# First adaptive-norm slice and input loaded in four column pairs, with row sums in four column quarters of PE

## The reference

```
ada = silu(c) @ W_ada[l] + b_ada[l]          # W_ada[l] is 1024 x 6144
sh1, sc1, g1, sh2, sc2, g2 = split(ada, 6)
u = x * (1 + sc1) + sh1
x = LayerNorm(alpha * x + (1 + g1) * Mixer(u))
u = x * (1 + sc2) + sh2
x = LayerNorm(alpha * x + (1 + g2) * SwiGLU(u))
```

## Time and profile before

| | us |
|---|---|
| median of 3 runs | 1724.36 |
| profiled execution, its own time | 1726.44 |
| its span | 1724.6 |
| PE busy | 1665.3 (97%) |
| DVE busy | 1017.7 (59%) |
| ACT busy | 630.8 (37%) |
| bytes moved | 192.05 MB, 111 GB/s |

### The profile page before, as it was taken

How to read it: one execution, slowest core, us unless ns; L and a number is a source line. 1 busy time by engine, 2 the same in 40 slices (tenths; PEclk the granted TensorE clock), 3 DMA queues, 4 the chain that set the end, 5 groups by cost and what they waited for, 6 DMA issues and landing times.

```text
span 1724.6 us, 21810 instructions
## 1 busy us (share of the span) xinstructions
PE 1665.3 (97%) x8561; PEld 1328.8 (77%) x8561; DVE 1017.7 (59%) x1620; ACT 630.8 (37%) x1146; POOL 51.4 (3%) x100
## 2 busy tenths in 40 slices
PE   6899999999999999999999999999999999999997
PEld 5778766677787888888878776666778788888886
DVE  4767578767675555554567656777567533333344
ACT  0532344544343322222253324454533533222222
POOL 2000000000000000000000000000000000000000
PEclk9899999999999999999999999999999999999997
DMA  9464322124326666655426231111233233333331
GB/s 325 131 183 138 83 62 62 37 86 134 113 72 198 180 183 184 194 165 161 141 82 170 79 86 50 38 25 35 65 98 98 62 97 98 97 98 101 91 100 49
DMA packets 269685, 192.05 MB, mean 111 GB/s; under 512 B 8168, under 2 KB 254480, under 8 KB 268560
## 3 DMA queue, kind: packets, MB, share of 16 engines
q1 hardware_dynamic: 255632, 147.94, 29.4%
q0 software_dynamic: 12032, 42.07, 8.2%
q10 hardware_dynamic: 1920, 0.66, 0.2%
HBM read 188.54 MB, written 2.10 MB: 111 GB/s over the span
## 4 chain that ended last, share of the span: by engine, by line
PE 89%; DVE 5%; DMA 2%; ACT 2%; issue 1%; SPq 0%; ACTq 0%; DVEq 0%
PE banks L1460 24%; PE banks L1462 23%; PE banks L1461 23%; PE banks L1576 4%; PE banks L1604 3%; PE banks L1630 2%; PE banks L1509 1%; PE banks L1510 1%; PE banks L1511 1%; PE banks L1578 1%; DMA ring<-in_w_in_dram 1%; DMA ada_first_a<-in_w_ada_dram 1%; PE banks L1664 1%; DVE w_lo L891 1%; PE banks L1524 1%
## 5 line engine op out<-in xcount | busy, mean ns | idle before, releaser
L1460 PE MATMUL banks<-u_hi,w_hi 128*128 128x512 f32 x1216 | 500.0, 411 | 10.3 <-DVE w_lo L891 7.6
L891 DVE TENSOR_TENSOR w_lo<-ring,w_hi 128x1024 fp32r<-128x1024 f32 (+2 forms) x246 | 294.4, 1199 | 316.6 <-ACT w_hi L632 315.7
L1462 PE MATMUL banks<-u_hi,w_lo 128*128 128x512 f32 x1216 | 476.2, 392 | 0.0
L1461 PE MATMUL banks<-u_lo,w_hi 128*128 128x512 f32 x1216 | 476.0, 391 | 0.0
L632 ACT ACTIVATE w_hi<-ring 128x1024 fp32r<-128x1024 f32 (+2 forms) x246 | 253.8, 1032 | 234.2 <-PE banks L1462 98.6
L1460 PEld LDWEIGHTS banks<-u_hi,w_hi 128*128 128x128 f32 x1216 | 230.1, 189 | 53.0 <-DVE w_lo L891 8.9
L1462 PEld LDWEIGHTS banks<-u_hi,w_lo 128*128 128x128 f32 x1216 | 229.2, 188 | 49.4
L1461 PEld LDWEIGHTS banks<-u_lo,w_hi 128*128 128x128 f32 x1216 | 230.5, 190 | 36.8
L779 ACT ACTIVATE probs<-banks,neg_max 128x128 f32<-128x128 f32 (+3 forms) x192 | 99.5, 523 | 168.4 <-DVE neg_max L1247 168.4
L1460 PE MATMUL banks<-h_hi,w_hi 128*128 128x512 f32 x352 | 138.5, 394 | 0.0
L1462 PE MATMUL banks<-h_hi,w_lo 128*128 128x512 f32 x352 | 137.0, 389 | 0.0
(11 more groups left out here) (225 smaller groups left out, 2098.6 us busy)
## 6 DMA issues: line engine op xcount, KB each, us to landing
ring<-in_w_ffn_in_dram SPq DMA_DIRECT2D x88, 512.0 KB, 3.9
ada_ring<-in_w_ada_dram POOLq DMA_DIRECT2D x80, 512.0 KB, 4.2
ring<-in_w_in_dram SPq DMA_DIRECT2D x72, 512.0 KB, 3.8
ring<-in_w_ffn_out_dram SPq DMA_DIRECT2D x32, 448.0 KB, 3.6
ring<-in_w_out_dram SPq DMA_DIRECT2D x16, 512.0 KB, 3.9
ring<-in_w_ffn_out_dram SPq DMA_DIRECT2D x16, 512.0 KB, 4.4
ada_first_a<-in_w_ada_dram SPq DMA_DIRECT2D x5, 1024.0 KB, 9.1
w<-in_cmp_w_k_dram SPq DMA_DIRECT2D x8, 512.0 KB, 4.9
```

Of the source, the lines that this page charges most:

```text
L891: V.tensor_tensor(lo, src, hi.bitcast(fp32), ALU.subtract).then_inc(split_lo, 1)
L1460: M(bank, wh[:, block], sh[:, k, :], start=start, stop=False)
L1461: M(bank, wh[:, block], sl[:, k, :], start=False, stop=False)
L1462: return M(bank, wl[:, block], sh[:, k, :], start=False, stop=stop)
```

## The change

The first 2048 columns of W_ada[0] and x are no longer loaded by rows of W_ada, but by four pairs of chunks. Pair j is x's 256 columns of chunks 2j and 2j + 1, and for the shift and the scale the 256 columns that belong to them, in two halves of 512 rows. The rows of these transfers are 1 KB long. kc and vc are loaded behind pair 0, ksl behind pair 1, kwn behind pair 2. The bias of the first 2048 columns comes with c and is turned with it.

DVE sums no slices any more. PE multiplies by a padded silu(c): 32 columns of which the first is silu(c) of one row block and the others zero (c_pad). Row block k = 4 * half + g goes to the g-th quarter of PE's columns and of the bank's partitions, 512 columns wide. ACT copies the bank (first_rows), and four column products of one column each bring the sums onto partitions and add the quarters. DVE adds the bias for the pair, and the two chunks of u are made. PE takes kc, vc and ksl together, chunk by chunk (`first_products`), between the row sums of the next pair. The turning of the vectors moves behind the last of these products, and DVE's copies of them, with POOL's start signal ahead of them, behind the last chunk. x is turned in three banks instead of six. The job parts w1 are loaded behind other jobs than before, after and not ahead of them.

```diff
-    order = [(0, "ada01")] + [(l, name) for l in range(DEPTH) for name in CHUNKS if name not in THIRD]
+    order = [(l, name) for l in range(DEPTH) for name in CHUNKS if name not in THIRD]
-W1_WITH = ["vsg0", "vsg1", "vsg2", "qn0", "qn1", "qn2", "qn3", "kd0"]
+W1_WITH = ["vsg1", "vsg2", "qn0", "qn0", "qn1", "qn1", "qn2", "qn3"]
...
+            def load_pair(j):
+                part = slice(2 * P * j, 2 * P * (j + 1))
+                sp.dma_start(x_tok[:, :, part], x[0, :, part].rearrange("(i p) n -> p i n", p=P)).then_inc(x_in[j], 16)
+                for half in range(2):
+                    rows = w_ada[0, 4 * P * half:4 * P * (half + 1), :]
+                    for a in range(2):
+                        src = rows[:, D_MODEL * a + 2 * P * j:D_MODEL * a + 2 * P * (j + 1)]
+                        sp.dma_start(ada_first[j][:, 4 * half:4 * half + 4, 2 * P * a:2 * P * (a + 1)],
+                                     src.rearrange("(k p) n -> p k n", p=P)).then_inc(first_in[2 * j + half], 16)
...
-            for k in range(KD):
-                if k >= 3:
-                    sp.wait_ge(first_in[k - 3], 16)
-                if k == 6:
-                    sp.dma_start(x_tok, x[0].rearrange("(i p) n -> p i n", p=P)).then_inc(x_in, 16)
-                sp.dma_start(ada_first[k], w_ada[0, k * P:(k + 1) * P, 0:2 * D_MODEL]).then_inc(first_in[k], 16)
-            for name in JOBS[:NS]:
-                load(0, name)
+            load_pair(0)
+            load(0, JOBS[0])
+            load(0, JOBS[1])
+            load_pair(1)
+            load(0, JOBS[2])
+            load_pair(2)
+            load(0, JOBS[3])
+            load_pair(3)
...
-            prepare(0, "kc")
-            prepare(0, "vc")
-            act.wait_ge(part1, 1)
-            for k in range(KD):
-                act.wait_ge(x_saved, k + 1)
-                sub_layer_input(0, k, banks[:, 2 + k % 6, :], mul_u[:, 0, k:k + 1], ada[:, 0, k:k + 1])
-                if k == 3:
+            for j in range(PAIRS):
+                act.wait_ge(rows_summed, j + 1)
+                nc.scalar.activation(first_rows, rows_ps, ACT.Copy).then_inc(rows_saved, 1)
+                if j == 0:
+                    prepare(0, "kc")
+                act.wait_ge(pair_ready, j + 1)
+                for k in (2 * j, 2 * j + 1):
+                    act.wait_ge(x_saved, k + 1)
+                    sub_layer_input(0, k, banks[:, 2 + k % 3, :], mul_u[:, 0, k:k + 1], ada[:, 0, k:k + 1])
+                if j == 0:
+                    prepare(0, "vc")
                     prepare(0, "ksl")
...
+            def first_pair(j):
+                at = ada[:, 0, 0:2 * KD].rearrange("p (a k) -> p a k", a=2)[:, :, 2 * j:2 * j + 2]
+                bias = vec[:, 0, 0:2 * KD].rearrange("p (a k) -> p a k", a=2)[:, :, 2 * j:2 * j + 2]
+                dve.wait_ge(cols_summed, j + 1)
+                link(V.tensor_tensor(at, cols_ps[:, 4 * j:4 * j + 4].rearrange("p (a k) -> p a k", a=2), bias, ALU.add))
+                V.tensor_scalar(mul_u[:, 0, 2 * j:2 * j + 2], ada[:, 0, KD + 2 * j:KD + 2 * j + 2], 1.0, None, ALU.add)\
+                    .then_inc(pair_ready, 1)
...
+            for j in range(PAIRS):
+                save_x(2 * j)
+                save_x(2 * j + 1)
+                first_pair(j)
+                if j == 0:
+                    prepare(0, "kc")
+                sub_layer_low(0, 2 * j)
+                sub_layer_low(0, 2 * j + 1)
+                if j == 0:
+                    prepare(0, "vc")
                     prepare(0, "ksl")
+            V.memset(d_mix[:, 0:1], 0.0).then_inc(part1, 1)
+            for l in range(DEPTH):
+                dve.wait_ge(vec_turned, l + 1)
+                link(V.tensor_copy(vec[:, l, :], banks[:, 2 + l, 0:V_ROWS]))
+                V.tensor_scalar(norm_s[:, l:l + 1], vec[:, l, V_NORM:V_NORM + 1],
+                                1.0 - LAMBDA_INIT[l], None, ALU.mult)
...
+            def turn_x(k):
+                pe.wait_ge(x_in[k // 2], 16)
+                if k >= 3:
+                    pe.wait_ge(u_ready, k - 2)
...
+            def sum_rows(j, half):
+                pe.wait_ge(first_in[2 * j + half], 32)
+                if j and not half:
+                    pe.wait_ge(rows_saved, j)
+                for g in range(4):
+                    k = 4 * half + g
+                    last = M(rows_ps[32 * g:32 * g + 32, :], c_pad[:, k, :], ada_first[j][:, k, :],
+                             start=half == 0, stop=half == 1)
+                if half:
+                    last.then_inc(rows_summed, 1)
+            def sum_columns(j):
+                pe.wait_ge(rows_saved, j + 1)
+                for m in range(4):
+                    last = M(cols_ps[:, 4 * j + m:4 * j + m + 1], first_rows[:, P * m:P * (m + 1)], one_col,
+                             start=True, stop=True)
+                last.then_inc(cols_summed, 1)
+            def first_products(k):
+                pe.wait_ge(u_ready, k + 1)
+                for name in FIRST:
+                    if k == 0:
+                        take_split(0, name)
+                    last = product(bank_of(0, name), split_slot(0, name), (u_hi, u_lo), k, k, k == 0, k == KD - 1)
+                    if k == KD - 1:
+                        done(0, name, last)
...
+            for j in range(PAIRS):
+                turn_x(2 * j)
+                sum_rows(j, 0)
+                if j:
+                    first_products(2 * j - 2)
+                turn_x(2 * j + 1)
+                sum_rows(j, 1)
+                sum_columns(j)
+                if j:
+                    first_products(2 * j - 1)
+            first_products(KD - 2)
+            first_products(KD - 1)
+            turn_vectors()
```

More of the change, by code:

```diff
@@ L168 @@
 ADA_SUM_LAYER = {g: int(name == "kwn") for name, g in ADA_SUM_WITH.items()}
-FIRST_DVE, FIRST_PE = (0, 2, 3, 5, 6, 7), (1, 4)
+FIRST = ("kc", "vc", "ksl")
+PAIRS = KD // 2
 ROW_LOADS, VEC_LOADS = 8 * DEPTH, 4 * DEPTH
@@ L273, in build @@
         x_tok = x_all[:, :, :].rearrange("p (i a) n -> p i (a n)", a=2)
[L274 to L277, removed]
+        c_rows = c_in_all[0:3 * KD, 0, 0:P]
         vec_rows = vec_in_all[0:V_ROWS, 0, 0:DEPTH * P].rearrange("p (l n) -> p l n", l=DEPTH)
@@ L337, in build @@
         nsa_ps, diff_ps = banks[:, 6, :], banks[:, 7, :]
+        rows_ps, cols_ps = banks[:, 6, :], banks[:, 7, 0:2 * KD]
         shift_ps, mean_col, var_col = banks[:, 2, :], banks[:, 3, 0:TT], banks[:, 4, 0:TT]
@@ L342, in build @@
         const_in = sem("const_in")
-        x_in = sem("x_in")
+        x_in = [sem(f"x_in{j}") for j in range(PAIRS)]
         vec_in = sem("vec_in")
@@ L609, in _ @@
             act.wait_ge(c_turned, 1)
-            nc.scalar.activation(c_silu[:, :], banks[:, 3, 0:KD], ACT.Silu).then_inc(c_ready, 1)
+            nc.scalar.activation(c_silu[:, :], banks[:, 3, 0:KD], ACT.Silu)
+            act.wait_ge(pad_clear, 1)
+            nc.scalar.activation(c_pad[:, :, 0], banks[:, 3, 0:KD], ACT.Silu).then_inc(c_ready, 1)
             for l in range(DEPTH):
@@ L901, in _ @@
             dve.wait_ge(c_ready, 1)
[L902 to L918, removed]
@@ L919, in _ @@
-            prepare(0, "kc")
-            prepare(0, "vc")
+            V.tensor_copy(vec[:, 0, 0:2 * KD], banks[:, 3, KD:3 * KD]).then_inc(vec_saved, 1)
             def save_x(k):
                 dve.wait_ge(x_turned, k + 1)
-                V.tensor_scalar(res[:, k, :], banks[:, 2 + k % 6, :], ALPHA, None, ALU.mult)\
+                V.tensor_scalar(res[:, k, :], banks[:, 2 + k % 3, :], ALPHA, None, ALU.mult)\
                     .then_inc(x_saved, 1)
-            for k in range(6):
-                save_x(k)
@@ L1382, in _ @@
             pe.wait_ge(ident_in, 16)
-            def first_slice(k):
-                pe.wait_ge(first_in[k], 16)
-                for m in range(2 * KD):
-                    M(bank_of(0, "ada01")[:, m:m + 1], ada_first[k][:, m * P:(m + 1) * P], c_silu[:, k:k + 1],
-                      start=False, stop=True, skip_group_check=True)
             def turn_vectors():
@@ L1393, in turn_vectors @@
                 for l in range(DEPTH):
[L1394 removed]
+                    nc.tensor.transpose(banks[:, 2 + l, 0:V_ROWS], vec_rows[:, l, :], ident[0:V_ROWS, 0:V_ROWS])\
                         .then_inc(vec_turned, 1)
[L1397 to L1409 removed]
@@ L1411, in _ @@
-            pe.wait_ge(c_loaded, 16)
-            nc.tensor.transpose(banks[:, 3, 0:KD], c_rows, ident[0:KD, 0:KD]).then_inc(c_turned, 1)
-            pe.wait_ge(zeros_ready, 1)
-            M(bank_of(0, "ada01")[:, 0:2 * KD], ident, zeros[:, :], start=True, stop=True)
-            pe.wait_ge(c_ready, 1)
-            for k in FIRST_PE:
-                first_slice(k)
-            turn_vectors()
-            turn_x(range(6))
-            pe.wait_ge(first_summed, 1)
-            for m in range(2 * KD):
-                last = M(bank_of(0, "ada01")[:, m:m + 1], first_sum[:, m * P:(m + 1) * P], one_col,
```

(12 more changed lines are left out.)

67 lines of the change are left out of this document (24 added, 43 removed).

## The result

The changed kernel takes 1730.63 us, the median of five runs, of which four lie from 1729.69 to 1733.73 and one, of 9286.23 us, is left out of the comparison. The kernel before took 1724.43 beside it (five runs, 1724.31 to 1725.04). The ratio is 1.0036, 95% interval 1.0021 to 1.005: slower by 6.2 us. The forecast was 1730.

A forecast was written before the change was run, and what follows sets the result against it. PE, busy 97% of the span, was taken as the bound. Its start's terms moved qn0 from 88.31 to 94.0, +5.7 us, giving 1732.1 for the profiled execution; with the median 2.1 lower, 1730, range 1722 to 1740.

The forecast's parts named there:

- the 94.0 of the sum: Forecast start of qn0, after which PE has no wait of weight; 88.31 before, so +5.7 us.
- Transfers: Start's loads in 1 KB rows at 345 GB/s: ksl lands at 28.3, last pair at 45.4, 7 to 11 us later.
- The wait for ksl's split: PE's order at block 0 stands until ACT and DVE have split ksl, at 30.8 us.
- Row sums: PE's padded products per pair, taken as four abreast: a group of 8 instructions 0.86 us at full clock, 1.7 low.
- PE's end of the three jobs: PE's last kc, vc and ksl products end at 62.6 us, with the clock rising at 41.0.
- Behind it: After the three jobs, setup delays ACT's copy of kc by 4.05 us, to 66.65 from 60.94; bounds 0.6 to 5.
- At nothing: Parts priced at zero: w1's later loads (1 to 2 us if one came late), shifted chunk numbers, POOL's first ring loads.
- POOL's later start: POOL's first ring loads wait for the last chunk but feed sums needed much later; priced at nothing.
- Serial row sums: Rival: row sums not four abreast; two abreast 5.1 us more, 1735; one after the other 15 more, 1745; chance 0.15.
- A transfer-bound start: Rival: transfers set the start's end, last pair at 41.5, 1718.6 us, only if ksl does not hold PE; chance 0.08.
- Full clock throughout with ksl split at 29: Rival: no low stretch of PE in the start, qn0 at 88.5, 1724.5 us; chance 0.22.
- The clock falling between groups: Rival: PE's pauses between each pair's long products lower the clock, 2.5 us a fall, two give 1735; chance 0.15.

The follow-up runs named there:

- both edits: Changed kernel with ksl taken whole behind kc and vc, and the vectors' turn and DVE's setup moved before the last chunk; 1722.49 us.
- products in the gap: Changed kernel with 13 useless 512-column products while PE waits for ksl's split; 1730.26 us, and 1729.7 when run again.
- best version: Changed kernel with ksl behind kc and vc, and vectors, lambdas and exp early, but v_cmp and casts behind the last chunk; 1718.51 us.

## Why the prediction was right, step by step

- *Direction and size.* +5.7 us was forecast from the moment qn0 starts, and +6.2 was measured between medians. In the profile itself qn0 is 3.65 us later than the 94.0 of the sum, and 2.1 us came back behind it, so the close agreement is in part luck. The profiled execution was also the slowest of the four, 3.1 us above their median, where the sum took off 2.1.
- *Transfers.* 345 GB/s for 1 KB rows: 343 to 348 measured. ksl landing at 28.3 and split at 30.8: the split began at 29.39 and ended at 31.8, 1.0 late. The last pair at 45.4: in the kernel with both edits its second half is taken up as it lands, at 46.45, again 1.0 late. The Trainium skill (DMA: Bandwidth & Descriptors, Specifications) has transfers at line rate from 512 bytes on, by which it would have been there at about 41; the trace does not agree: 46.45, and 343 against 408 GB/s for 8 KB rows.
- *The wait for ksl's split.* Right in place and length (a gap until 31.83, ended by DVE's split), and shown to be the largest cost by the kernel without it: 5.2 of 8.0 us are gained by pair 1's column sums, and the low stretch is gone with the stop.
- *Row sums.* Four abreast was right, though the group takes 1.07 and 1.94 us instead of 0.86 and 1.7. The Trainium skill (TensorEngine Tiling (Array Packing), Key Properties) says that a change of tiling mode drains the engine; 0.2 us a group is the most that it could have cost here, and no run separates it from the latency of the last instruction.
- *PE's end of the three jobs.* The mis-sized term: 66.7 instead of 62.6. 1.0 is the later split. 2.0 is an estimate for the clock, which rose at 45.0 and not at 41 (4 us more at half speed). The rest is PE's work per pair: 9.1 us where the sum had 8.4, twice. These make 4.4 for the 4.1 measured. The clock's course was also another than the sum's. It had PE at the low level all the way to 41, by one place where the clock rose 5 us after the first products. The trace has the full level at 27.83, 1.4 us after the first product, a fall with the stop for ksl, and a rise at 45.0, 13.2 us after the restart. That the low stretch ended within 4 us of the 41 is luck, as the profiles in which it lasted 3.4 us show.
- *Behind it.* The gap before kwn, put at 9 to 10 us, was 8.85, and the 4.05 us from PE's end to ACT's copy were 3.6. Both costs were shown by the kernels that take them away: the gap became 4.32 with the setup earlier, 3.38 with ksl behind, and none with both.
- *At nothing.* w1's placement: shown, to within the 2 us by which medians of like kernels differ. POOL's later start was not tried.
- *The rivals.* Serial row sums cost 15 us (forecast 15; measured 1745.6 in all) and don't happen. A transfer-bound start comes only once ksl is out of the way, as its condition said: 1718.5 is the time that this rival gave, in a kernel without ksl's wait, though not by its sum: its terms, 41.5 and what stands behind, add to 50.3 and not to 51.3, the last pair came at 46.45 and not at 41.5, and the transfers are worth 1 us. Full clock throughout with ksl split at 29 was priced at 1724.5. The kernel with products in the gap had the clock, up to the end of the three jobs, but not the early ksl, and measured 1730. The clock falling between groups, priced at two falls and 1735, happened in another place: not in the pauses of 0.72 us for ACT's copy, where it stayed at 1.00 from 45 us on, but at the stop for ksl, which the sum had at the low level anyway.

What stays open: how much of the 6 us is clock, and why the low stretch behind the stop lasts 3.4 us in one execution and 13.6 in another. Medians of like kernels differ by 2 us and single executions by 4, and the profile shows one execution of each.

## What to carry to other kernels

When work is made to advance piece by piece as data lands, put into the piece-wise set only what is ready when the first piece is, since one late operand holds the engine's whole order; and price what the removed tail was covering (here kwn's split and DVE's setup). Moving a step earlier moves its waits too: look up where in the queue its data is before it goes in front of the work that counts. And find the one event after which the distance to the end does not change (here ACT's copy of kc); an experiment is then read from one row.

## What the runs showed of the hardware

- Four f32 products of 32 columns by 512 in the four quarters of PE run side by side: 8 instructions in 1.07 us at 2.4 GHz and 1.94 at 1.2, against 3.62 in one quarter at 2.4 GHz.
- A stop of PE of 2.4 to 3.2 us while the clock stood at its full level (the wait for ksl) brought a stretch at 1.2 GHz in all five profiles that have it: 3.4 us in three, 10.2 in one, and 13.6 in one, in which PE was busy 12.45 us. Nothing in the kernels tells the five apart. A stop of 3.7 us at the full clock (both edits, pair 3) brought a fall to 0.52 for 6.8 us. Pauses of 0.7 to 1.2 us (ACT's copy, the last pair's transfer) brought none.
- The clock column of the changed kernel's profile read 1.00 at 21 to 25 us while durations there are those of the low level (row sums 1.94 us at 24.59). In the profile of the best version the same stretch reads 0.50. Where a profile has no fall or rise on record yet, the duration is to be trusted, and not the column.
